# Expert rows gathered and spread by 0/1 products on the TensorE, 32 places a pass, 4 MB weight transfers into 4 slots, router and token rows made during w_out

## The reference

```python
h = h + mixed @ w_out[layer]
h = h + hierarchical_moe(rmsnorm(h, norm_ffn_w[layer]), ...)
return rmsnorm(h, final_norm_w)[:, N_META:]

# hierarchical_moe, of each token t (n_tok = 272):
g_prob = softmax(t @ w_group + b_group); g_sel = argmax(g_prob); g_gate = max(g_prob)
e_logits = (t @ w_router[g_sel]) + b_router[g_sel]          # 8 experts of the chosen group
top_v, top_i = lax.top_k(e_logits, 2)
top_w = softmax(top_v) * g_gate
out[t] = sum over the two e of top_w * ((silu(t @ w1[e]) * (t @ w3[e])) @ w2[e])
# w1, w3: (32, 2048, 512), w2: (32, 512, 2048): 12.58 MB an expert, 402.65 MB in all
```

## Time and profile before

| | |
|---|---|
| median of 3 runs | 1681.1 us (1680.99 to 1681.78) |
| the profiled execution's own time | 1683.12 us |
| its span in the trace | 1681.4 us |
| PE busy | 1452.1 us, 86% of the span |
| DVE, ACT, POOL busy | 285.2, 250.5, 88.9 us |
| moved by DMA | 495.83 MB, of which 192 expert transfers of 2 MB |
| granted clock of TensorE, mean | 0.928 |

### The profile page before, as it was taken

The page is one execution under the profiler, slowest core; times in us unless marked ns, Lnnn a source line. Parts: engine busy times, 40 slices in busy tenths (PEclk is TensorE's granted clock), DMA queues, the critical chain, the costliest instruction groups (busy, mean ns, idle before and its releaser), DMA issues.

```text
span 1681.4 us, 16119 instructions
## 1 busy us (share of the span) xinstructions
PE 1452.1 (86%) x6416; PEld 806.2 (48%) x6416; DVE 285.2 (17%) x714; ACT 250.5 (15%) x396; POOL 88.9 (5%) x172
## 2 busy tenths in 40 slices
PE   6999999999998997888878888788788788887881
PEld 3888888777886784433323323223233232232230
DVE  4312542341211014121000000000000000000003
ACT  2112413112150012210000100000001001000002
POOL 2000000000000000010000100100000001000000
PEclk9999999999999999898989989989889899898896
DMA  6343354334332565699999999999999999999994
GB/s 160 100 150 100 101 130 128 101 101 133 118 100 86 164 241 213 248 426 427 428 427 426 427 425 423 423 411 412 424 414 417 424 416 425 418 414 421 415 409 171
DMA packets 125982, 495.83 MB, mean 295 GB/s; under 512 B 27988, under 2 KB 97752, under 8 KB 99928
## 3 DMA queue, kind: packets, MB, share of 16 engines
q1 hardware_dynamic: 115536, 482.98, 72.4%
q0 software_dynamic: 9216, 8.94, 1.5%
q10 hardware_dynamic: 1192, 3.37, 0.6%
HBM read 498.79 MB, written 21.10 MB: 309 GB/s over the span
## 4 chain that ended last, share of the span: by engine, by line
PE 57%; DMA 39%; DVE 1%; ACT 1%; SPq 1%; issue 1%; POOLq 0%; ACTq 0%; DVEq 0%
DMA ring<-in_moe_w_dram 37%; PE bank L1239 24%; PE bank L1582 18%; PE bank L1282 7%; PE bank L1321 1%; DMA ring<-in_w_out_dram 1%; PE bank L1299 1%; PE bank L1250 1%; SPq L446 1%; PE bank L1293 1%; PE bank L1603 1%; PE bank L1267 1%; DMA ring<-in_x_dram 1%; PE bank L1371 1%; PE bank L1519 0%
## 5 line engine op out<-in xcount | busy, mean ns | idle before, releaser
L1582 PE MATMUL bank<-ring,proj 128*64 128x512 f32 x2048 | 530.4, 677 | 160.4 <-DMA ring<-in_moe_w_dram 159.5
L1582 PEld LDWEIGHTS bank<-ring,proj 128*64 128x64 f32 x2048 | 183.0, 156 | 487.1 <-issue 486.0
L1239 PE MATMUL bank<-uT,ring 128*128 128x272 f32 x1664 | 390.3, 394 | 0.0
L1239 PEld LDWEIGHTS bank<-uT,ring 128*128 128x128 f32 x1664 | 313.5, 190 | 64.4 <-issue 1.5
L1603 PE MATMUL bank<-ring,proj 128*64 128x512 f32 x1024 | 227.0, 595 | 1.3 <-DVE proj L1187 0.9
L1603 PEld LDWEIGHTS bank<-ring,proj 128*64 128x64 f32 x1024 | 71.1, 137 | 135.0 <-issue 132.3
L1182 DVE COPY proj<-bank 128x512 f32<-128x512 f32 x32 | 22.1, 692 | 665.4 <-PE bank L1569 665.4
L820 ACT ACTIVATE proj<-bank 128x512 f32<-128x512 f32 x32 | 34.5, 1079 | 674.2 <-PE bank L1582 674.2
L1282 PE MATMUL bank<-proj,ring 128*128 128x272 f32 x512 | 122.8, 404 | 9.2 <-DMA ring<-in_w_out_dram 9.2
L1282 PEld LDWEIGHTS bank<-proj,ring 128*128 128x128 f32 x512 | 100.4, 197 | 31.4 <-DMA ring<-in_w_out_dram 10.0
L640 ACT ACTIVATE proj<-bank 128x272 f32<-128x272 f32 x52 | 20.7, 397 | 296.1 <-PE bank L1239 296.1
(11 more groups left out here) (294 smaller groups left out, 706.4 us busy)
## 6 DMA issues: line engine op xcount, KB each, us to landing
ring<-in_moe_w_dram SPq DMA_DIRECT2D x192, 2048.0 KB, 20.3
ring<-in_w_in_dram SPq DMA_DIRECT2D x26, 2048.0 KB, 8.2
ring<-in_w_out_dram SPq DMA_DIRECT2D x8, 2048.0 KB, 8.1
ring<-expert_rows SPq DMA_DIRECT2D x4, 1024.0 KB, 8.2
tokens_normed<-proj ACTq DMA_DIRECT2D x2, 1024.0 KB, 3.9
out_dram<-ring SPq DMA_DIRECT2D x2, 1024.0 KB, 3.9
ring<-in_x_dram SPq DMA_DIRECT2D x1, 1024.0 KB, 8.3
uT<-in_final_norm_w_dram ACTq DMA_DIRECT2D x1, 1024.0 KB, 4.6
```

Of the source, the lines that this page charges most:

```text
L1239: last = V.matmul(outs, a, b, start=start and j == 0, stop=stop and j == n - 1)
L1582: last = V.matmul(pb[2][64 * g:64 * g + 64, :], xsT[:, c, part, :], w[:, c, :], start=part + c == 0, stop=part == 1 and c == 7)
```

## The change

It does these things:

1. An expert takes 32 places a pass (`CAP`), 256 tokens instead of 272 (the 16 meta tokens have no output and are left out from `w_out` on), and further passes if more than 32 tokens choose it.
2. Tokens are gathered on PE: `tokens` multiplies a 0/1 matrix (made by DVE from the ranks `RK`, and scaled by the token's inverse root) by the token rows `u2`, which stay in SBUF. Four column groups of the array work on four quarters of 512 columns. The rows are turned (`turn_tokens`), and the product with w1 is a sum of 4 matmuls in each of 4 column groups of 32 columns; the four partial sums are added while they are turned (`turn_hidden`, with the 0/1 matrix `selq`).
3. `down` writes the four quarters of an expert's output rows in four column groups; `combine` multiplies them by the weights' 0/1 matrix (turned by `spread`), and DVE adds each 128 x 512 result to `h2` in SBUF (`sums`). There are no indirect DMAs, no `tokens_normed` or `expert_rows` in HBM any more.
4. The weights come in transfers of 4 MB (a whole w1, w3 or w2) into 4 slots; the fourth slot lies over the end of `hT` and the start of `proj`. The first two are issued among the chunks of `w_out`.
5. `w_out` is done tile by tile on 256 tokens; only the first two tiles are split around `norm_done`. Behind each tile PE turns the tile before into token rows and adds its part of the logits (`by_rows`). ACT squares and copies the turned rows, POOL multiplies them by the norm's weights.
6. The last norm: POOL multiplies by the final weights, ACT squares each quarter as soon as it is summed, the output leaves in four transfers of 0.5 MB.

```diff
-    CAP = 64
+    CAP = 32
+    QR = P // CAP
+        E_AT = (2 * SLOT, 4 * SLOT, 0, RING + KD * T)
...
@@ SP
+                if 2 * c == NIN + 2:
+                    sp.wait_ge(s["norm_done"], 1)
+                    sp.dma_start(eslot(0), matrix(0, 0)).then_inc(m_in[0], 16)
+                if 2 * c == NIN + 6:
+                    sp.dma_start(eslot(1), matrix(0, 1)).then_inc(m_in[1], 16)
+            sp.wait_ge(s["in_tile"], NIN + NOUT)
+            sp.dma_start(eslot(2), matrix(0, 2)).then_inc(m_in[2], 16)
+            sp.wait_ge(s["t_ps"], 4 * NA)
+            sp.wait_ge(s["lg_ready"], 1)
+            sp.dma_start(eslot(3), matrix(1, 0)).then_inc(m_in[3], 16)
+            used = (s["h1_ps"], s["h3_ps"], s["y_ps"])
+            for m in range(4, 16):
+                sp.wait_ge(used[(m - 4) % 3], (m - 4) // 3 + 1)
+                sp.dma_start(eslot(m % 4), matrix(m // 3, m % 3)).then_inc(m_in[m % 4], 16)
...
@@ POOL
-                V.indirect_dma_start(out=xs, out_offset=None, in_=u2d[:, :], ...
-                V.indirect_dma_start(out=yd[:, :], ...
+            for g in range(4):
+                for a in range(NA):
+                    V.tensor_tensor(u2[:, a, :]..., h2[:, a, g * 512:(g + 1) * 512]..., nwrow..., ALU.mult)
+            for a in range(NA):
+                for d in range(4):
+                    pool.wait_ge(s["y_acc"], count * 8 + (8 * (NE - 1) + 4 * a + d + 1))
+                    V.tensor_tensor(fout[:, a, d * 512:(d + 1) * 512], h2..., fw..., ALU.mult)
...
@@ DVE
+            def sums(n, first=False):
+                for j in range(8):
+                    a, d = j // 4, j % 4
+                    dve.wait_ge(s["cb_ps"], n * 8 + (j + 1))
+                    V.tensor_tensor(h2[:, a, d * 512:(d + 1) * 512], h2[:, a, d * 512:(d + 1) * 512],
+                                    pb[6 + j % 2][:, :], ALU.add).then_inc(s["y_acc"], 1)
...
@@ PE
+            def by_rows(k):
+                for a in range(NA):
+                    last = V.transpose(pb[5 + a][...], hT[:, k, NM + a * P:NM + (a + 1) * P], ident[:, :])
+                for a in range(NA):
+                    last = V.matmul(pb[(4, 7)[a]][:, 0:LG], hT[:, k, NM + a * P:NM + (a + 1) * P], wr[:, k, :], ...)
+            def tokens(n):
+                for a in range(NA):
+                    for g in range(QR):
+                        last = V.matmul(pb[0][CAP * g:CAP * (g + 1), :], oh[:, a, :], u2[:, a, g * 512:(g + 1) * 512], ...)
+            def up(n, slots, counts):
+                for r in range(2):
+                    for j in range(4):
+                        for g in range(QR):
+                            last = V.matmul(pb[2 + r][CAP * g:CAP * (g + 1), :], xsT[:, j, g, :], w[:, 4 * g + j, :],
+                                            start=j == 0, stop=j == 3)
+            def combine(n, first=False):
+                for j in range(8):
+                    a, g = j // 4, j % 4
+                    if not first or j >= 2:
+                        pe.wait_ge(s["y_acc"], n * 8 + (j - 1))
+                    V.matmul(pb[6 + j % 2][:, :], wT[CAP * g:CAP * (g + 1), a * P:(a + 1) * P],
+                             ysb[CAP * g:CAP * (g + 1), :], start=True, stop=True).then_inc(s["cb_ps"], 1)
+            def one(n, at, last=False, first=False):
+                up(...); tokens(n + 1); turn_hidden(n); turn_tokens(n + 1)
+                combine(n - 1); spread(n); down(n, *at[2])
```

862 lines of the change are left out of this document (397 added, 465 removed).

## The result

| | before | after |
|---|---|---|
| time, median (all runs) | 1681.21 us (1680.99 to 1681.78) | 1586.38 us (1584.45 to 1588.34, 4 runs) |
| ratio | | 0.9435, 95% interval 0.9419 to 0.9452 |
| span and own time of the profiled execution | 1681.4, 1683.12 | 1582.6, 1584.61 |

The prediction was 1585 us, range 1568 to 1648. The four times of the changed kernel lie in two pairs, 1584.5 and 1588.2; the profile is of one of the lower pair.

What follows compares the result with a forecast made beforehand. The prediction took the expert stage to be bound by the weight stream: first slot freed at 655.0, plus 1.0 and 908 us of stream to 1564, plus 21.3 us of end, gives 1585 us, range 1568 to 1648.

Steps and rivals of the forecast that it cites:

- the pieces of the forecast: Savings over the whole span: first slot freed 34 us earlier, fourth slot 10, rate 37, end 15; together 95 us.
- `combine` over 8 us: Sign of being wrong, in the expert loop: `combine` was forecast at 6.0 us an expert.
- `w_out` and logits done: Start 507.0, products 112.9 us, `by_rows` 12.5, last add 1; both chunk waits go; ends at 633.4 against 638.9.
- The stretch to the first slot: From `w_out` to the first freed slot: 16.6 us of routing and tokens, about 5 of first `up`; free at 655.0.
- The doubt about POOL's products: In the routing: POOL's last two token-row products may hold up DVE by up to 2.4 us.
- The stream: Expert weights: 92 transfers of 4.19 MB at 9.87 us, 908 us (904 to 941), ending at 1564 us.
- That the larger transfers neither help nor hurt is assumed: Expert weight stream: transfers of 4.19 MB were taken to leave the rate as it was, 426 GB/s with weights alone.
- PE in the loop: PE work an expert: 112 packed instructions at 0.115 us, `combine` 6.0; sum 23.3 us, 6.3 below the stream.
- PE just above the stream: Rival, expert loop: thin work lowers the clock, PE takes 31.5 us an expert; 1644 us (1605 to 1690), chance 0.11.
- The end: After the last byte: `down` 4, copy 0.6, sums 6.0, then last norm and output; 21.3 us (17 to 28).
- Four groups no better than two: Rival, packed products in the loop: 0.222 us each, PE 37.5 us an expert, slower at 1830 us; chance 0.06.
- the rate that stays: Rival, expert stream: period stays 30.7 us though gathers are gone; 941 us, 1618 us in all; chance 0.08.

Runs made afterwards that it cites:

- experiment 1: Kernel before the change, without the loop's gathers and scatters, its last stage reading other rows of the same size: 1645.01 us, ratio 0.9782.
- experiment 3: Changed kernel with the first two expert matrices asked for only after `w_out` instead of among its chunks: 1601.12 us, ratio 0.9517.
- experiment 5: Changed kernel without the `combine` products and DVE sums of experts 0 to 30, those of expert 31 kept: 1582.24 us, ratio 0.939.
- experiment 6: Changed kernel with the products of `tokens` made four times over for each expert: 1681.63 us, ratio 0.9988.
- experiment 10: Changed kernel with the last two of eight products for the token rows on DVE instead of POOL: 1582.57 us, ratio 0.9413.
- experiment 2: Changed kernel with each 4 MB weight transfer issued as two of 2 MB: 1591.09 us, ratio 0.9469.
- experiment 8: Changed kernel with `down` between the previous expert's `combine` pairs and the first half's squares reduced between the last sums: 1585.84 us, ratio 0.9415.
- experiment 7: Changed kernel with the `down` product made between the pairs of the previous expert's `combine`: 1585.04 us, ratio 0.942.
- experiment 9: Changed kernel with sixteen unused PE products ahead of the ranks and two ahead of the first tokens: 1582.79 us, ratio 0.941.
- experiment 11: Changed kernel with experiments 7, 9 (ten products for sixteen) and 10 together, plus unused products between those of the last two combines: 1599.91 us, ratio 0.9512.

## Why the prediction was right, step by step

The time came within 1.4 us of the forecast, and the account of it (bound by the stream; it starts earlier, stops less and flows faster) is what experiments 1, 3, 5 and 6 show. In the pieces of the forecast (34 us from the first slot, 10 from the fourth, 37 from the rate, 15 from the end) the spans give 40, 10, 47 and 2. That the number is so close is luck: the last weights landed 15.6 us before their forecast, and what follows them took 12.9 us longer. One of the prediction's signs of being wrong came true as well: `combine` over 8 us.

| Step | predicted | measured |
|---|---|---|
| `w_out` and logits done | 633.4 | about 628.1 |
| from there to the first freed slot | 21.6 us | 21.2 us (649.36) |
| standstill of the queue, inside the row above | 3 us (1 to 8) | about 2.5 (half the rate in 645 to 650) |
| one transfer of 4.19 MB in the loop | 9.87 us, 426 GB/s | 9.71 us, 432 GB/s |
| from the first freed slot to the last byte | 909 us | 899 us |
| last weights landed | 1564 | 1548.4 |
| PE an expert | 23.3 us | 27.0 us (29.14 less 2.1, experiment 6) |
| from there to the end of the span | 21.3 us | 34.2 us |
| span | 1585 | 1582.6 |

- **`w_out`: right in kind, 5 us too long.** A tile takes 7.57 us (612.19 to 619.76). Its products are 6.99 us, 0.218 each, as summed; `by_rows` adds 0.58 where I took 0.78. That gives 3.2 us over sixteen, the products 1.1, and 1 I had put behind the logits for a last add, which `by_rows` of the tile before covers (L1471 from 626.80, the add of 0.42 us from 626.78). Both chunk waits went, and the expert's transfer ahead of the third chunk cost nothing.
- **The stretch to the first slot: right in sum, by parts that shifted.** The doubt about POOL's products (up to 2.4 us) was the right one: they cost 2.6 us, shown by experiment 10, and not by running slowly but by making two small operations wait. The first `up` ran at full clock in this profile, the first tokens at half.
- **The stream: right, the rate 1.5% too low.** "That the larger transfers neither help nor hurt is assumed" was the part of this step that failed; experiment 2 gives them 6 of the 10 us by which the stream was shorter. The other part was that weights without gathers flow at 428 GB/s (experiment 1) and not at the 426 of one 10 us window. The indirect transfers were 0.23 MB an expert (0.74 MB in 100 us), not 0.3; the sum does not use that size. The Trainium skill ("DMA: Bandwidth & Descriptors", Specifications) has about 358 GB/s for a core, as half of what a stack of HBM gives two. The 432 of this trace, with one core at work, lie above it, so the forecast was right not to take that share as a bound.
- **PE in the loop: the packed products right, two terms missed.** 0.114 us against 0.115. An instruction of 512 columns alone would take 0.437 us, an estimate (6.99 us for 32 of 256 columns, doubled), so four groups ran at 3.8 times one. The Trainium skill ("TensorE: Matmul & The Clock Gate", Part 3) has 2.38 for three, and its loss doesn't show here. The mis-sized terms are `combine`, 9.7 us for 6.0, and `down`, 5.1 to 5.8 for 3.7. DVE's add takes 0.69 us as computed, but the step "with the handshake 0.75, eight 6.0 us" took PE to be ready each time, and it failed twice. First, with two PSUM banks a product waits for the sum two before it, so a pair costs about the time of its products and one add: 1.90 us at the full clock, 7.6 for the eight. Second, the clock falls on the way (0.66 over the combine in the loop, 0.54 and 0.50 in the rows of 1545 to 1549), a pair then comes every 2.85 us, and `down` starts at the lower level. About 1.6 of the 3.7 us are the first, 2.1 the second. Against them stands a term that was too large: of the 1.5 us for copies that PE waits for and changes of the array's split nothing shows in the rows of one expert. So the margin of 6.3 us was in truth 2.1 (experiment 6). The rival "PE just above the stream" was closer than its 0.11 said.
- **The end: the largest error, 13 us.** I let PE be ready when the last weights landed. It isn't: it trails by 6.4 us (1548.4 to 1554.83), in the combine of the expert before; without those combines the tail is 5.7 us shorter (experiment 5). Then `down` takes 5.7 for 4 and the sums 10 for 6 (1561.20 to 1571.28). From the last sum on it was 11.3 us, predicted 10.7. POOL was hidden as assumed (9.84 us from 1563.19, beside the sums).
- **The rivals.** Four groups no better than two, and the rate that stays, are refuted by 0.114 us and by experiment 1. No further pass was made (96 transfers of 4 MB in the trace, three for each of 32 experts).

Open stays what parts the times of the changed kernel by 3.7 us. The clock of the first `up` is one cause: the profiles of the changed kernel and of experiments 2, 3 and 8 free the first slot at 649.05 to 649.62, those of 5 and 7, with the same start, at 653.72 and 653.21, behind a first `up` of 10.02 and 9.87 us against 7.08. But with the clock held in experiment 9 a spread of 4.3 us remained.

## What to carry to other kernels

When the last transfer of a stream lands, the engine behind it is often not idle but behind by the thin work that the stream hid: count it into the tail, and at the clock that thin work leaves. Where two engines hand two buffers back and forth, price a pair as one engine's time for it plus one step of the other, not as the slower engine's time alone. In a stream-bound loop a cheaper step buys nothing until the end; what moves the time is when the first buffer is freed, and there small operations that wait for another engine and a TensorE at its lower clock cost about 3 us each here. To keep TensorE's clock up, extra products paid where it stood idle anyway (experiment 9) and a kernel that had them between small products that could run side by side was 13.5 us slower (experiment 11).
